# Removing the unread products with the unit matrix between pooling and the expert stage

## What is computed

```
h = _modulate(x, norm_g[l, 0], sh1, sc1)
mix = _pool_mixer(h, pool_w[l // 2], pool_scale[l // 2])
x = x + gt1 * mix
h = _modulate(x, norm_g[l, 1], sh2, sc2)
...
logits = (h @ w_router).astype(jnp.float32)
top_v, top_i = lax.top_k(logits, TOP_K)
top_w = jax.nn.softmax(top_v, axis=-1)
gates = jnp.sum(jax.nn.one_hot(top_i, N_EXP) * top_w[..., None], axis=-2)
for e in range(N_EXP):
    out = out + gates[..., e:e + 1] * _swiglu(h, w_gate[e], w_up[e], w_down[e])
```

## Time and profile before

| | us |
|---|---|
| median of 3 runs | 1379.74 |
| lowest, highest | 1378.78, 1380.05 |
| the profiled execution, time | 1380.04 |
| the profiled execution, span of the trace | 1378.3 |
| pooling products to the start of the expert stage, in the span | 508.2 to 535.95 |
| expert stage, in the span | 535.95 to 1366.3 |

### The profile page before, as it was taken

How to read it: one execution, slowest core, us unless ns; L and a number is a source line. 1 busy time by engine, 2 the same in 40 slices (tenths; PEclk the granted TensorE clock), 3 DMA queues, 4 the chain that set the end, 5 groups by cost and what they waited for, 6 DMA issues and landing times.

```text
span 1378.3 us, 23298 instructions
## 1 busy us (share of the span) xinstructions
PE 1338.7 (97%) x10242; PEld 705.6 (51%) x10242; DVE 400.3 (29%) x517; ACT 282.4 (20%) x364; POOL 108.3 (8%) x182
## 2 busy tenths in 40 slices
PE   4999999999999999999999999999999999999987
PEld 2997677678888885333333333333333333333332
DVE  2856344666444454101201400401101100100213
ACT  2673534453344333000000000000000000000011
POOL 6200141324000001000000000000000000010010
PEclk9999999999999999999999999999999999999998
DMA  9854967988777779999999999999999999999995
GB/s 382 306 161 152 379 252 277 405 311 301 244 244 245 260 293 416 363 360 427 427 423 430 427 422 412 424 410 430 424 426 429 425 425 427 428 423 427 425 428 239
DMA packets 103750, 499.86 MB, mean 363 GB/s; under 512 B 10514, under 2 KB 14303, under 8 KB 74855
## 3 DMA queue, kind: packets, MB, share of 16 engines
q1 hardware_dynamic: 87664, 471.75, 84.7%
q10 hardware_dynamic: 13590, 18.29, 3.7%
q0 software_dynamic: 2400, 8.42, 1.5%
HBM read 478.74 MB, written 19.69 MB: 362 GB/s over the span
## 4 chain that ended last, share of the span: by engine, by line
PE 92%; DMA 4%; DVE 2%; ACT 1%; issue 1%; ACTq 0%; DVEq 0%; SPq 0%
PE ps L2523 21%; PE ps L2520 17%; PE ps L2550 15%; PE ps L458 5%; PE ps L460 5%; PE ps L459 5%; PE ps L2557 4%; DMA ring_a<-in_moe_down 3%; PE ps L1927 3%; PE ps L1913 2%; PE ps L2059 1%; PE ps L2060 1%; PE ps L2061 1%; PE ps L2203 1%; PE ps L2016 1%; DMA raw<-in_w_mod 1%
## 5 line engine op out<-in xcount | busy, mean ns | idle before, releaser
L399 DVE TENSOR_TENSOR w_lo<-raw,w_hi 128x2048 fp32r<-128x2048 f32 x60 | 144.8, 2416 | 124.2 <-ACT w_hi L395 124.2
L2523 PE MATMUL ps<-ring_a,hTf 128*32 128x512 f32 (+1 forms) x1488 | 146.7, 551 | 0.0
L395 ACT ACTIVATE w_hi<-raw 128x2048 fp32r<-128x2048 f32 x59 | 112.8, 1914 | 108.7 <-PE ps L460 99.8
L2520 PE MATMUL ps<-raw,hTf 128*64 128x512 f32 (+1 forms) x624 | 123.8, 552 | 0.9 <-DMA raw<-in_moe_up 0.9
L1862 DVE TENSOR_TENSOR hm<-gate_bc,ps 32x384 f32<-32x384 f32 (+1 forms) x56 | 34.0, 607 | 267.5 <-PE ps L2520 266.6
L1868 DVE TENSOR_TENSOR hm<-gate_bc,ps 128x384 f32<-128x384 f32 (+1 forms) x16 | 9.4, 588 | 345.5 <-PE ps L2523 345.3
L2523 PEld LDWEIGHTS ps<-ring_a,hTf 128*32 128x32 f32 x1488 | 47.9, 110 | 96.9 <-issue 93.9
L458 PE MATMUL ps<-w_hi,hTh 128*128 128x512 f32 x232 | 91.5, 394 | 0.0
L460 PE MATMUL ps<-w_lo,hTh 128*128 128x512 f32 x232 | 90.4, 389 | 0.0
L459 PE MATMUL ps<-w_hi,hTl 128*128 128x512 f32 x232 | 90.3, 389 | 0.0
L2520 PEld LDWEIGHTS ps<-raw,hTf 128*64 128x64 f32 x624 | 44.1, 137 | 78.0 <-issue 74.9
(11 more groups left out here) (429 smaller groups left out, 1776.1 us busy)
## 6 DMA issues: line engine op xcount, KB each, us to landing
raw<-in_w_mod SPq DMA_DIRECT2D x48, 1024.0 KB, 7.8
raw<-in_moe_down SPq DMA_DIRECT2D x22, 2048.0 KB, 22.6
ring_a<-in_moe_down SPq DMA_DIRECT2D x20, 2048.0 KB, 19.1
ring_a<-in_moe_up SPq DMA_DIRECT2D x14, 2048.0 KB, 18.8
raw<-in_moe_gate SPq DMA_DIRECT2D x13, 2048.0 KB, 18.3
ring_b<-in_moe_down SPq DMA_DIRECT2D x13, 2048.0 KB, 19.5
ring_a<-in_moe_gate SPq DMA_DIRECT2D x11, 2048.0 KB, 24.6
raw<-in_moe_up SPq DMA_DIRECT2D x10, 2048.0 KB, 15.5
```

Source lines behind the costliest of these rows:

```text
L395: nc.scalar.activation(w_hi[:, w % SPLIT], raw[:, slot % RAW], ACT.Copy).then_inc(s["hi_ready"], 1)
L399: nc.vector.tensor_tensor(w_lo[:, w % SPLIT], raw[:, slot % RAW], w_hi[:, w % SPLIT].bitcast(F32), ALU.subtract).then_inc(s["lo_ready"], 1)
L2520: last = MM(ps[HB * j:HB * j + HB, part % 4, 0:w], xT[:, kt, HB * (g // 2):HB * (g // 2) + HB], wt[:, kt % 2, 2 * (g % 2) + j, :], start=k ...
L2523: last = MM(ps[TOK * j:TOK * j + TOK, part % 4, 0:w], xT[:, KT * g + kt], wt[:, kt % 2, j, :], start=kt == 0, stop=kt == KT - 1)
```

## The change

The helper and its four calls are taken out: two products after pooling, two after the turns of the second norm, one after `turn_tokens(1)`, and one before the gather. The waits around them stay. Nothing is moved and nothing is added. On the other engines no instruction differs.

```diff
             pool_mix(1, 1)
-            def keep_busy(n, rows, bank=3):
-
-                for _ in range(n):
-                    MM(ps[:, bank, :], ident[:, :], flat(rows), start=True, stop=True)
-
             pe.wait_ge(s["yp_by_scalar"], 2)
-            keep_busy(2, band)
             turn_xn(2, 2, xn1)
-            keep_busy(2, band)
 
             pe.wait_ge(s["hT_by_vector"], 6)
             pe.wait_ge(s["hT_by_scalar"], 6)
...
             turn_tokens(1)
-            keep_busy(1, hTf1[:, 0:2])
             pe.wait_ge(s["mask_ready"], 1)
...
             turn_gates(3, 3, 0)
-            keep_busy(1, hTf1[:, 0:2], 2)
             pe.wait_ge(s["tokens_saved"], 2)
             gather(0)
```

## The result

The changed kernel takes 1384.65 us in the median of six runs (1383.90 to 1388.66), the kernel before 1379.89 us in the same comparison (1378.78 to 1381.29). The ratio is 1.0039 with a 95% interval of 1.0029 to 1.0048: slower by 4.8 us, outside the predicted range of 1379.3 to 1383.0. On another chip eleven runs gave 1384.08 us against 1380.16 us, a ratio of 1.0026 (1.0017 to 1.0035). The profiled execution took 1384.45 us, with a span of 1382.7 us.

The account below looks back on a forecast made before the run. TensorE, busy for 97% of the span, was taken as the bound, with loads that have no reserve. Work -0.1 and one clock fall +1.3 gave +1.2 on 1379.74, so 1380.9 us, range 1379.3 to 1383.0.

Parts of the forecast that it names:

- The work that leaves is worth nothing: From pooling to the gather, the removed passes themselves save between 0 and 0.22 us, taken as -0.1.
- rival D: Between pooling and the gather, the chain is right and 3.44 us go: 1376.3 us, chance 0.02.
- The pauses: TensorE pauses about 2.3 us ahead of the second turns, formerly 0.69, and 1.65 us ahead of the router product.
- The clock falls once, for at most 1.65 us: Between pooling and the gather, one clock fall costs 0.94 to 1.65 us, taken as 1.3; chance 0.45.
- rival B: The clock falls twice, the second time in the gather at the full 1.65 us: 1382.6 us, chance 0.21.
- The evidence for a clock that holds: Near the start, 18 to 22 us, the clock stayed at 1.00 with a longest pause of 1.79 us.
- Rival A: The clock stays up after pooling, so only the work counts: 1379.6 us, chance 0.20 shared with E.
- E: Load slack keeps the delay from reaching the end: 1379.6 to 1379.9 us, chance 0.20 shared with Rival A.
- Rival C: The clock stays low from the second turns to the expert stage: about 1386.5 us, chance 0.07.
- A delay reaches the end whole: A delay or gain at the expert stage's start, 535.95, counts at full size, since the loads have no reserve.
- The end as a neutral part: Behind the start of L2523, the trace stays the old one, later by the same 1 to 2 us.

Follow-up runs that it names:

- place 4: Kernel before with only the one unread product ahead of the gather taken out: ratio 0.9999 (0.9990 to 1.0008).
- place 1: Kernel before with only the two products ahead of the second norm's turns taken out, run twice: ratios 0.9997 and 1.0003.
- further trace 3: Third of three more profiles of the whole change, all six products out: 1384.76 us, against 1380.04 in the trace of the kernel before.
- place 2: Kernel before with only the two products behind the second norm's turns taken out: ratio 1.0009 (0.9998 to 1.0019).
- its end filled: Kernel before plus two unread products ahead of each of four units of the last expert's down projection, run twice: ratios 0.9993 and 1.0004.

## Why the prediction was wrong, point by point

**The work that leaves is worth nothing: right.** From pooling to the second turns it is 8.62 us in both kernels, to the router product 11.36 before and 11.35 after. Without place 4, and without place 1 in the trace that has no fall, the gather starts 17.76 us after pooling, as before. I had allowed 0 to -0.22 and took -0.1; it is 0. The 3.44 us of the chain, rival D, were a place where TensorE was seen, not work that anyone waited for.

**The pauses: right.** 2.20 and 1.64 us, said 2.3 and 1.65.

**The clock falls once, for at most 1.65 us: the step that failed.** Two terms in it were wrong. The first is the price. I took it from the end of the kernel, where a group of dense products ran 1.65 us longer and was then back at 2.4 GHz, and used it as an upper bound. Ahead of the gather the first fall cost 2.03 us in four of the six traces of the change, 1.39 in one and 3.06 in another; the gather alone lost 2.74 us in one kernel. What follows a pause here is turns, small products and more pauses, and the clock stays low for longer. That it is this which holds it low is argued and not shown. The second is the number of falls. Two were the usual case and not one: rival B, to which I gave 0.21. Its sum of 2.85 us was near the 3.08 to 3.09 us measured ahead of the expert stage in four of six traces, but by luck: it had 1.3 us for the first fall and 1.65 for the second, and they measured 2.03 and 1.05. The place of the second is right: in the kernel without the last two places the clock is low in the gather, behind the five products of eight columns.

**The evidence for a clock that holds: one execution.** That the clock stayed at 1.00 behind a pause of 1.79 us near the kernel's start, in code that the change doesn't touch, was taken as the pause that leaves the clock up. The kernel after, at the same place:

```profile
21.65 1.81 PE L1927 MATMUL ps<-raw,vecs 128*32 128x512 f32 x8 [1.65 <-DMA raw<-in_w_mod]
```

Here the eight passes took 1.81 us for 1.06, behind a shorter pause, and the mean granted clock from 20 to 24 us is 0.73. In seven of the eighteen traces of all kernels they took 1.57 to 1.94 us, behind pauses of 1.44 to 1.98 us; in the other eleven 1.06 or 1.07, behind pauses of 1.46 to 1.86. So the 1.79 us bound nothing, and the sixteen turns behind them (2.85 us here for 1.97) said nothing on turns either. These falls are ahead of pooling and cost nothing that the intervals above would show, but they are in the mean clocks.

**Rival A**, that the clock stays up, was given 0.20 with E. It is out for the whole change, but it was not idle: with place 1 alone out it is what one of the two traces shows. **Rival C**, a low clock all the way, was given 0.07 and priced at 6.8 us; it is further trace 3, which lost 5.35 us. The Trainium skill (TensorE: Matmul & The Clock Gate, "Why this matters for your kernels") warns of idle gaps over about 3 us. By that advice the clock would have held here; it fell behind pauses of 2.20 and 1.64 us, and it held behind the one of 3.59 us, so neither way was the length a limit.

**A delay reaches the end whole: right.** The five added products show it, and the loads of the kernel after, 2.4 us late at 543.92 and at 1317.53.

**The end as a neutral part: not safe.** I counted from 535.95 to the end as fixed. It varies between 841.5 and 844.6 us from trace to trace: by 1.7 us as a fall lies ahead of a wait for a load or after the last one, and by 1 us or more with the moment at which the last load is there. Of the 4.8 us, 1.0 to 2.0 are of this kind (2.00 in the profiled execution). A range for a kernel that ends so needs 2 us for that alone.

## What to carry to other kernels

Before you take out work that nobody reads, look at what the clock did around it: if it fills pauses (here of 2.20 and 1.64 us) in a chain of short dependent steps, it may be worth more than it costs, here six products of 0.86 us, which cost nothing, for some 4 us. Price a fall of the clock by the kind of work that runs behind it, and allow that all of it takes twice its time; one fall behind which dense products run is no upper bound. And look at more than one trace before you take a clock that held as a rule. And when work in the chain that ended last goes, ask what the next step waited for: here each was within 0.12 us of its operand, and nothing was won.

## What the runs showed of the hardware

The pause alone does not decide: the same pause of 2.20 us in the same kernel was followed by a fall in one trace and by none in another, one of 1.64 us was followed by a fall in the kernel without place 2, and one of 3.59 us, for a load, by none in the kernel without place 4. A low clock can last while TensorE works: in further trace 3 the rows stay at 0.50 from 530 to 538, with TensorE busy for 4.00 and 3.49 us of the two times 4. Float32 transposes of 128 columns kept the clock at 1.00 from 518 to 542 us in the trace of the kernel that has them in place of the products. And a kernel with its end filled, at a mean clock of 0.9986 or 0.9989, was no faster than one at 0.9969 or 0.9970: in its traces TensorE still waits 0.2 to 0.6 us for loads in the last units.
